# Cell stage of a two-layer block: selector rows in the free half, first split on VectorE, weighing ahead of scoring

## The chip, the cores and the metric

One NeuronCore of one Trainium2 chip runs the whole program in one launch. The metric is device time in microseconds (us) of that core. The engines are TensorE (PE), VectorE (DVE), ScalarE (ACT), GpSimd (POOL) and SyncE (SP, which only issues transfers here).

## The reference

Two transformer blocks at 512 tokens and width 1024, in fp32. The first has forgetting attention, chunked attention, memory attention and a gated feed forward; the second has an mLSTM layer, a multi-head latent attention layer and two squared-ReLU feed forwards. The change touches only the mLSTM mixer. Its recurrence over chunks is equal to one masked product over all 512 tokens, and that is what the kernel computes for each of 8 heads:

```
bb = cumsum(log_sigmoid(f));  m_t = running max over s<=t, in log space
w[t,s] = exp(bb_t - bb_s + i_s - m_t)   for s <= t, else 0
s[t,s] = (q_t . k_s) * w[t,s]
h_t    = sum_s s[t,s] v_s / max(|sum_s s[t,s]|, exp(-m_t))
out    = (rmsnorm(h) * sigmoid(og)) @ w_out
```

q and k have 64 columns per head, v has 128.

## The kernel before

All fp32 products are made of reduced-precision pieces: an operand is split into a high part (fp32r, rounded by ACT) and a low part (the difference), and `three` (L631 to L635) issues high x high, high x low and low x high. Weights come as 314 panels of 128x1024: SP loads a panel into `stage`, ACT makes `WH` (L1076), POOL makes `WL` (L528), PE uses them.

The cell stage lies between the projection "a_in" (queries, keys, output gate, values) and the projection "a_out". It runs over 8 heads n and, in each, over 4 blocks of 128 keys kb. A step is s = 4n + kb; its width is 512 - 128 kb query columns (512, 384, 256, 128), because later keys are seen by fewer queries. For each step:

- PE `cell_scores(s)` (L949): three matmuls of keys by queries into `G[s%2]`, contraction over 64 rows (rows 0 to 63 for an even head, 64 to 127 for an odd one); one matmul that spreads the head's running-maximum row, `SELC[0:40]` by `RB[0:40]`, into `T[s%2]` (L960); one matmul identity by `maskTr`, 128 columns (L961), which adds the causal mask.
- ACT `cell_exp(s)` (L1388): exponent of `T` into `sq`. DVE `cell_probs(s)` (L1928): `t` = `G` times `sq`.
- ACT `cell_pt_high(s)` (L1396) and then the low part of the weights into `CPT`: for kb = 0 on POOL (`first_low`, L576), else on DVE (`cell_pt_low`, L1934).
- PE `cell_weigh(s)` (L970): three matmuls of values by weights into `O[0]` (L633 to L635) and two of ones by weights into `O[1]` (L985), contraction over 128 rows.

Once for each head: PE `cell_guard` (L967, exp(-m) row, `SELC[64:104]` by `RB[64:104]`) and ACT `cell_guard_exp` (L1400); after the fourth weighing ACT `cell_square` (L1407 and L1410), DVE `cell_take` (L1941, frees `O[0]`), PE `cell_mean` (L993, two passes' worth of fp32 records), DVE `cell_den` (L1945) and `cell_sum` (L1950), ACT `cell_root` (L1414 logarithm, L1418 exponent), POOL `gate` (L581), DVE `cell_norm` (L1955), ACT `cell_high` (L1422), POOL `out_low` (L585). The banks `O[0]` and `O[1]` are single, so the first weighing of a head waits for `cell_take` and `cell_square` of the head before.

The order on each engine is written by hand; every engine works its list strictly from the front, and a wait blocks what is behind it. PE's list is in the code printed below. ACT's, for step s: [kb=1: square of head n-1], `pt_high(s)`, `exp(s+2)`, [kb=2: `guard_exp(n)`], [kb=3: `root(n-1)`], [kb=2: `high(n-2)`]. DVE's: [kb=1: `take(n-1)`], `probs(s+1)`, `pt_low(s)` (kb > 0), [kb=2: `den(n-1)`], [kb=3: `sum(n-1)`], [kb=1: `norm(n-2)`]. POOL's, for head n: `first_low(n)`, `out_low(n-2)`, `gate(n-1)`.

Behind the stage, `project` "a_out" starts with chunks 0 and 1, whose input rows are the heads' outputs, k = 0 to 6 first and k = 7 last. SP issues the load of the positions (into `apiece`, which overlaps `CW`) and the a_out panels 2 and on only when `out_low` of the last head is done.

## Time and profile before

| what | value |
|---|---|
| median of 3 runs | 2446.33 us (2441.97 to 2459.98) |
| profiled execution | 2446.78 us, of which the span from the first to the last instruction is 2445.0 us |
| mean granted TensorE clock over the span | 0.952 |
| PE / DVE / ACT / POOL busy | 92% / 48% / 36% / 40% |

A busy PE is not a PE at full rate: TensorE is granted 1.2 or 2.4 GHz, and the view of stretches prints the mean of that as a share of 2.4 GHz (0.50 is 1.2 GHz). Timeline rows give start, duration, engine, line, operation, output<-input and shape; in brackets stands the idle time of the engine before the row and who ended it. Matmul records overlap, because they are pipelined: the distance between two starts is what a matmul costs in a stream.

### The profile page before, as it was taken

Reading aid. Unit: us, or ns where it says so; the run is one execution under the profiler, and the core shown is the slowest. Engines: PE = TensorE matmul, PEld = TensorE weight load, DVE = VectorE, ACT = ScalarE, POOL = GpSimd, SP = SyncE. Lnnn points to the kernel's source line nnn. Section 1 sums busy time; section 2 is a strip of 40 time slices with the busy share of each in tenths; the row PEclk is TensorE's granted clock in tenths of the full one; section 3 lists DMA queues with packets and bytes.
Section 4 is the critical chain, followed back from the end, with each engine's and each line's share of the span. In section 5 each row is a group of like instructions: output and inputs, shape, how many; then the busy total and the mean of one; then the engine's idle time right before and its main releaser. Section 6 shows DMA issues by size and latency. Waiting matters only on the chain.

```text
span 2445.0 us, 27598 instructions
## 1 busy us (share of the span) xinstructions
PE 2245.8 (92%) x9514; PEld 1728.7 (71%) x9514; DVE 1174.7 (48%) x1669; ACT 888.8 (36%) x1449; POOL 976.9 (40%) x499
## 2 busy tenths in 40 slices
PE   6999968699899999899998899999977998999997
PEld 4777756577688888576666688888655776888885
DVE  4745544523555556763444643343553336434435
ACT  4226653343322222333344433223345444322332
POOL 2436624453344444333323344444324543444443
PEclk9999979799999999999868999999989899999999
DMA  5750022211144444255201122222212001222222
GB/s 194 254 192 18 7 98 86 78 60 61 52 155 154 161 158 154 103 198 174 76 1 48 51 95 94 94 94 94 69 44 69 26 27 49 91 92 93 94 94 78
DMA packets 66599, 234.25 MB, mean 96 GB/s; under 512 B 7136, under 2 KB 8416, under 8 KB 66400
## 3 DMA queue, kind: packets, MB, share of 16 engines
q1 hardware_dynamic: 66528, 233.33, 28.6%
q8 instruction: 41, 0.67, 0.1%
q14 instruction: 30, 0.25, 0.0%
HBM read 231.20 MB, written 2.10 MB: 95 GB/s over the span
## 4 chain that ended last, share of the span: by engine, by line
PE 76%; issue 8%; DVE 7%; ACT 5%; POOL 3%; DMA 1%; SPq 0%; POOLq 0%; DVEq 0%; ACTq 0%
PE bank L633 24%; PE bank L635 22%; PE bank L634 22%; POOL WL L528 2%; PE bank L705 2%; DVE acc L1554 1%; DVE Y L1579 1%; PE bank L748 1%; ACT sq L1090 1%; DVE H L1575 1%; DVE apiece L1629 1%; DMA apiece<-ada 1%; ACT WH L1076 1%; DVE Y L1618 1%; PE bank L690 1%
## 5 line engine op out<-in xcount | busy, mean ns | idle before, releaser
L528 POOL TENSOR_TENSOR WL<-stage,WH 128x1024 fp32r<-128x1024 f32 x314 | 763.7, 2433 | 1233.8 <-ACT WH L1076 1233.8
L1076 ACT ACTIVATE WH<-stage 128x1024 fp32r<-128x1024 f32 x314 | 332.6, 1060 | 1108.3 <-PE bank L635 1072.2
L633 PE MATMUL bank<-H,WH 128*128 128x512 f32 x1524 | 616.8, 405 | 58.3 <-DVE H L1575 32.2
L634 PE MATMUL bank<-H,WH 128*128 128x512 f32 x1524 | 608.6, 399 | 0.0
L635 PE MATMUL bank<-H,WL 128*128 128x512 f32 x1524 | 608.6, 399 | 0.0
L633 PEld LDWEIGHTS bank<-H,WH 128*128 128x128 f32 x1524 | 290.0, 190 | 156.0 <-issue 43.3
L635 PEld LDWEIGHTS bank<-H,WL 128*128 128x128 f32 x1524 | 290.0, 190 | 70.6
L634 PEld LDWEIGHTS bank<-H,WH 128*128 128x128 f32 x1524 | 290.7, 191 | 66.6 <-issue 0.8
L633 PE MATMUL bank<-HID,WH 128*128 128x512 f32 x688 | 272.9, 397 | 5.2 <-DVE Y L1758 5.2
L1758 DVE TENSOR_TENSOR Y<-bank,Y 128x512 f32<-128x512 f32 x344 | 226.0, 684 | 107.6 <-PE bank L635 106.5
L634 PE MATMUL bank<-HID,WH 128*128 128x512 f32 x688 | 272.8, 397 | 0.0
L635 PE MATMUL bank<-HID,WL 128*128 128x512 f32 x688 | 272.7, 396 | 0.0
L1629 DVE SCALAR_TENSOR_TENSOR apiece<-apiece,cond 128x1024 f32<-128x1024 f32 x112 | 189.2, 1703 | 108.3 <-DMA apiece<-ada 108.2
L1744 DVE SCALAR_TENSOR_TENSOR t<-bank,t 128x512 f32<-128x512 f32 x64 | 44.3, 692 | 286.3 <-ACT t L1230 286.2
L1748 DVE TENSOR_TENSOR HID<-t,HID 128x512 fp32r<-128x512 f32 x86 | 125.8, 1462 | 66.5 <-ACT HID L1235 66.5
L633 PEld LDWEIGHTS bank<-HID,WH 128*128 128x128 f32 x688 | 129.8, 189 | 36.9 <-issue 5.6
L635 PEld LDWEIGHTS bank<-HID,WL 128*128 128x128 f32 x688 | 129.7, 189 | 31.5
L634 PEld LDWEIGHTS bank<-HID,WH 128*128 128x128 f32 x688 | 129.7, 189 | 31.3
L1554 DVE TENSOR_TENSOR acc<-acc,sq 128x512 f32<-128x512 f32 (+1 forms) x59 | 89.7, 1520 | 101.0 <-ACT sq L1090 100.7
L1703 DVE TENSOR_TENSOR PT<-bank,PT 128x128 fp32r<-128x128 f32 (+2 forms) x112 | 54.0, 482 | 78.3 <-ACT PT L1190 78.1
L556 POOL TENSOR_SCALAR sq<-sq,stat 128x384 f32<-128x384 f32 (+2 forms) x56 | 74.2, 1336 | 21.1 <-DVE stat L1696 21.1
L1690 DVE TENSOR_REDUCE stat<-bank 128x1 f32<-128x128 f32 (+2 forms) x112 | 53.6, 479 | 50.0 <-PE bank L815 21.7
(257 smaller groups left out, 2777.0 us busy)
## 6 DMA issues: line engine op xcount, KB each, us to landing
stage<-panels SPq DMA_DIRECT2D x314, 512.0 KB, 3.5
apiece<-ada SPq DMA_DIRECT2D x112, 512.0 KB, 4.3
x<-xT SPq DMA_DIRECT2D x4, 1024.0 KB, 6.9
outT<-x SPq DMA_DIRECT2D x8, 256.0 KB, 2.1
Y<-bias SPq DMA_DIRECT2D x1, 1024.0 KB, 4.8
V<-memT SPq DMA_DIRECT2D x2, 512.0 KB, 4.4
con<-cons SPq DMA_DIRECT2D x1, 517.0 KB, 6.3
cond<-c SPq DMA_DIRECT2D x1, 512.0 KB, 9.1
```

The lines of the kernel that those rows point to most:

```text
L528: pool.tensor_tensor(WL[:, slot, :], stage[:, slot, :], WH[:, slot, :].bitcast(F32), ALU.subtract).then_inc(s_split, 1)
L556: pool.tensor_scalar(prob[qb][:, 0:w], prob[qb][:, 0:w], stat[:, 8 + qb:9 + qb], None, ALU.mult)\
L633: pe.matmul(out, wh, rh, start=start, stop=False)
L634: pe.matmul(out, wh, rl, start=False, stop=False)
L635: return pe.matmul(out, wl, rh, start=False, stop=stop)
L1076: act.activation(WH[:, slot, :], stage[:, slot, :], ACT.Copy).then_inc(s_hisplit, 1)
L1554: dve.tensor_tensor(acc[:, 0:width], first, sq[:, m % 2, 0:width], ALU.add).then_inc(s_add, 1)
L1629: dve.scalar_tensor_tensor(apiece[:, k % 2, :], apiece[:, k % 2, :], 1.0, cond[:], ALU.mult, ALU.mult, accum_out=adac[:, column]).then_inc ...
L1690: dve.tensor_reduce(stat[:, qb:qb + 1], score_bank[qb][:, 0:keys_of(name, qb)], AX, ALU.max, negate=True)\
L1703: dve.tensor_tensor(lo, T[qb % 2][:, 0:w].rearrange("p (k q) -> p k q", q=P), hi.bitcast(F32), ALU.subtract).then_inc(sm["pt_split"], 1)
L1748: dve.tensor_tensor(HID[:, slot, j, 1, :], t[:, j, :], HID[:, slot, j, 0, :].bitcast(F32), ALU.subtract).then_inc(sm["split"], 1)
L1758: dve.tensor_tensor(Y[:, m, :], (T + O)[m % 4][:, :], Y[:, m, :], ALU.add)\
```

## The change

1. **Free half.** The selector matmul of `cell_scores` takes `SELC` and `RB` rows of the half that the head's keys don't use: rows 64 to 103 for an even head, 0 to 39 for an odd one. It is issued second, between the first and the second key matmul. So `RB[64:104]` now holds a copy of the maximum rows, and the guard rows move to a new tile `RG` (rows 0 to 39). To make room, `wgate` is placed over `V`, `maskTr` goes (the one mask tile `maskr` is rewritten before and after the cells), `MR` goes.
2. **First split on DVE.** `first_low` leaves POOL; `cell_pt_low` runs for all four kb on DVE. `cell_norm` leaves DVE for POOL, whose list is now `gate(n)`, `norm(n)`, `out_low(n)`, head by head.
3. **PE order.** In each step PE issues `cell_weigh(s-1)`, then the mean if it is due, then `cell_scores(s+2)`, then the guard; before, `cell_scores(s+2)`, guard, mean, `cell_weigh(s-1)`.
4. **Warm matmuls.** In each of the first two steps four matmuls of 512 columns into `O[1]` are added, whose result nobody uses (`warm`, L687), and PE waits for all value low parts ahead of the loop.

ACT's list in the cells is unchanged. The diff, cut to what the prediction speaks of:

```diff
@@ -571,27 +570,24 @@
             def cells():
-                def first_low(n):
-                    pool.wait_ge(cell["pt_high"], 4 * n + 1)
-                    pool.tensor_tensor(CPT[:, 1, 0, :], t[:, 0, :], CPT[:, 0, 0, :].bitcast(F32), ALU.subtract)\
-                        .then_inc(cell["pt_low_first"], 1)
-
                 def gate(n):
                     pool.wait_ge(cell["root"], n + 1)
                     pool.tensor_tensor(rstd[:, :], rstd[:, :], QK[:, 8 + n, :], ALU.mult).then_inc(cell["gated"], 1)
+
+                def norm(n):
+                    pool.wait_ge(cell["gated"], n + 1)
+                    pool.tensor_tensor(CW[:, 2 + n % 2, :], CW[:, 2 + n % 2, :], rstd[:, :], ALU.mult)\
+                        .then_inc(cell["normed"], 1)
                 def out_low(n):
                     pool.wait_ge(cell["high"], n + 1)
                     pool.tensor_tensor(H[:, n, 1, :], CW[:, 2 + n % 2, :], H[:, n, 0, :].bitcast(F32), ALU.subtract)\
                         .then_inc(cell["split"], 1)
-                for n in range(HEADS + 2):
-                    if n < HEADS:
-                        first_low(n)
-                    if n >= 2:
-                        out_low(n - 2)
-                    if 1 <= n <= HEADS:
-                        gate(n - 1)
+                for n in range(HEADS):
+                    gate(n)
+                    norm(n)
+                    out_low(n)
             split_lows(0, PANEL0["mem_k"] + 2)
             attention("self")
...
@@ -955,29 +952,31 @@
                     pe.wait_ge(s_vlow, NT + 2)
                 if s >= 2:
                     await_bank_pair(pe, s)
-                three(G[s % 2][:, 0:w], QKH[rows, 4 + n // 2, keys], QKL[rows, 4 + n // 2, keys],
-                      QKH[rows, n // 2, kb * P:S], QKL[rows, n // 2, kb * P:S], True, True)
-                pe.matmul(T[s % 2][:, 0:w], SELC[0:40, n * P:(n + 1) * P], RB[0:40, kb * P:S], start=True, stop=False)
-                pe.matmul(T[s % 2][:, 0:P], identr[:, :], maskTr[:, :], start=False, stop=True)\
-                    .then_inc(cell["scores"], 1)
+                gates, out = gate_rows[1 - n % 2], T[s % 2]
+                sel = SELC[gates, n * P:(n + 1) * P]
+                kh, kl = QKH[rows, 4 + n // 2, keys], QKL[rows, 4 + n // 2, keys]
+                qh, ql = QKH[rows, n // 2, kb * P:S], QKL[rows, n // 2, kb * P:S]
+                pe.matmul(G[s % 2][:, 0:w], kh, qh, start=True, stop=False)
+                pe.matmul(out[:, 0:w], sel, RB[gates, kb * P:S], start=True, stop=False)
+                pe.matmul(G[s % 2][:, 0:w], kh, ql, start=False, stop=False)
+                pe.matmul(G[s % 2][:, 0:w], kl, qh, start=False, stop=True)
+                pe.matmul(out[:, 0:P], identr[:, :], maskr[:, :], start=False, stop=True).then_inc(cell["scores"], 1)
             def cell_guard(n):
                 if n:
                     pe.wait_ge(cell["guard_exp"], n)
-                pe.matmul(AD[:, :], SELC[64:104, n * P:(n + 1) * P], RB[64:104, :], start=True, stop=True)\
+                pe.matmul(AD[:, :], SELC[0:40, n * P:(n + 1) * P], RG[:, :], start=True, stop=True)\
                     .then_inc(cell["guard"], 1)
             def cell_weigh(s):
                 n, kb = s // 4, s % 4
+                pe.wait_ge(cell["pt_low"], s + 1)
                 if kb == 0:
-                    pe.wait_ge(cell["pt_low_first"], n + 1)
                     if n:
                         pe.wait_ge(cell["num"], n)
                         pe.wait_ge(cell["den_square"], n)
                     else:
                         pe.wait_ge(s_vlow, 2 * NT)
-                else:
-                    pe.wait_ge(cell["pt_low"], 3 * n + kb)
                 at = slice(n * P, (n + 1) * P)
                 three(O[0][:, kb * P:S], VH[:, kb, at], VL[:, kb, at],
                       CPT[:, 0, kb, kb * P:S], CPT[:, 1, kb, kb * P:S], kb == 0, kb == NT - 1)
...
@@ -994,15 +993,18 @@
             cell_scores(0)
             cell_scores(1)
+            pe.wait_ge(s_vlow, 2 * NT)
             for s in range(4 * HEADS):
+                if s < 2:
+                    warm(O[1], 4)
+                if s:
+                    cell_weigh(s - 1)
+                if s % 4 == 2 and s >= 4:
+                    cell_mean(s // 4 - 1)
                 if s + 2 < 4 * HEADS:
                     cell_scores(s + 2)
                 if s % 4 == 0:
                     cell_guard(s // 4)
-                if s % 4 == 2 and s >= 4:
-                    cell_mean(s // 4 - 1)
-                if s:
-                    cell_weigh(s - 1)
             cell_weigh(4 * HEADS - 1)
             cell_mean(HEADS - 1)
...
@@ -1371,13 +1373,14 @@
             evacuate_high("a_in", lambda c: QKH[:, c, :], lambda c: 1.0 if c // 4 % 2 else 64 ** -0.5)
             evacuate("a_og", 8, lambda c: QK[:, c + 8, :], func=ACT.Sigmoid)
             load_ln_exp()
+            act.activation(maskr[:], con[:, CON["maskT"]:CON["maskT"] + P], ACT.Copy).then_inc(s_cr, 1)
             logit_rows(1, 16)
             evacuate_half(PANEL0["a_in"] + 16, 0, 1, VH)
             act.wait_ge(s_scan, 1)
+            act.activation(RB[64:72, :], t[0:8, 0, :], ACT.Copy)
             act.activation(RB[0:8, :], t[0:8, 0, :], ACT.Copy).then_inc(s_rb, 1)
             act.wait_ge(s_scan, 2)
-            act.activation(RB[64:72, :], CW[0:8, 2, :], ACT.Copy)
-            act.activation(MR[:, :], CW[0:8, 2, :], ACT.Copy).then_inc(s_rb, 1)
+            act.activation(RG[0:8, :], CW[0:8, 2, :], ACT.Copy).then_inc(s_rb, 1)
             evacuate_half(PANEL0["a_in"] + 16, 1, None, VH)
             def cell_exp(s):
...
@@ -1908,8 +1913,9 @@
             chain.link(dve.tensor_copy(gs[:], ST[:, 0:8 * NT].rearrange("p (a b) -> p a b", b=8)))
             dve.wait_ge(s_rb, 2)
             dve.tensor_tensor(RB[32:40, :], t[0:8, 0, :], RB[0:8, :].bitcast(F32), ALU.subtract)
+            dve.tensor_tensor(RB[96:104, :], t[0:8, 0, :], RB[0:8, :].bitcast(F32), ALU.subtract)
             dve.wait_ge(s_rb, 3)
-            dve.tensor_tensor(RB[96:104, :], CW[0:8, 2, :], MR[:, :].bitcast(F32), ALU.subtract).then_inc(s_rbl, 1)
+            dve.tensor_tensor(RG[32:40, :], CW[0:8, 2, :], RG[0:8, :].bitcast(F32), ALU.subtract).then_inc(s_rbl, 1)
             for n in range(HEADS):
                 last = dve.tensor_scalar(SELC[:, n * P:(n + 1) * P], ones[0:104, :],
                                          con[0:104, CON["minus_onehot"] + n:CON["minus_onehot"] + n + 1], None,
...
@@ -1920,10 +1926,7 @@
             def cell_probs(s):
                 n, kb = s // 4, s % 4
                 if s >= 2:
-                    if (s - 2) % 4 == 0:
-                        dve.wait_ge(cell["pt_low_first"], (s - 2) // 4 + 1)
-                    else:
-                        dve.wait_ge(cell["pt_low"], (s - 2) // 4 * 3 + (s - 2) % 4)
+                    dve.wait_ge(cell["pt_low"], s - 1)
                 dve.wait_ge(cell["exp"], s + 1)
                 dve.tensor_tensor(t[:, s % 2, 0:S - kb * P], G[s % 2][:, 0:S - kb * P], sq[:, s % 2, 0:S - kb * P],
                                   ALU.mult).then_inc(cell["probs"], 1)
...
@@ -1949,11 +1952,6 @@
                 dve.wait_ge(cell["mean"], n + 1)
                 dve.scalar_tensor_tensor(CW[:, n % 2, :], ST[:, :], 1.0 / P, CW[:, n % 2, :], ALU.mult, ALU.add)\
                     .then_inc(cell["sum"], 1)
-
-            def cell_norm(n):
-                dve.wait_ge(cell["gated"], n + 1)
-                dve.tensor_tensor(CW[:, 2 + n % 2, :], CW[:, 2 + n % 2, :], rstd[:, :], ALU.mult)\
-                    .then_inc(cell["normed"], 1)
             steps = 4 * HEADS
             cell_probs(0)
...
@@ -1963,14 +1961,12 @@
                     cell_take(n - 1)
                 if s + 1 < steps:
                     cell_probs(s + 1)
-                if kb and s < steps:
+                if s < steps:
                     cell_pt_low(s)
                 if kb == 2 and 1 <= n <= HEADS:
                     cell_den(n - 1)
                 if kb == 3 and 1 <= n <= HEADS:
                     cell_sum(n - 1)
-                if kb == 1 and n >= 2:
-                    cell_norm(n - 2)
             dve.wait_ge(s_pos, 16)
             chain.link(dve.tensor_copy(ropeF, apiece[:].bitcast(I32)[:, 0, 0:S]))
```

## Rows read from the trace of the kernel before

**Rows 1.** View of stretches: us, busy of PE, PEld, DVE, ACT, POOL, clock, DMA share, GB/s.

```profile
1204.00:1308.60 104.60, 97.65 (x342) 66.49 (x342) 48.74 (x86) 52.06 (x109) 27.05 (x22) 0.69 0.00 1
...
1236.00:1239.00 3.00, 3.00 (x7) 1.54 (x7) 1.03 (x3) 0.62 (x2) 0.00 (x0) 0.50 0.03 5
```

**Rows 2.** Timeline of PE: a head's first weighing, first and last of seven.

```profile
1221.11 0.47 PE L633 MATMUL bank<-CPT,VH 128*128 128x512 f32 x1 [0.79 <-DVE CW L1941]
...
1301.72 0.79 PE L633 MATMUL bank<-CPT,VH 128*128 128x512 f32 x1 [1.90 <-POOL CPT L576]
```

**Rows 3.** Timeline of ACT, from the exponent of step 28 to the square.

```profile
1293.85 0.69 ACT L1388 ACTIVATE sq<-bank,gs 128x512 f32<-128x512 f32 x1 [3.52 <-PE bank L961]
...
1295.01 0.63 ACT L1422 ACTIVATE H<-CW 128x512 fp32r<-128x512 f32 x1
1295.53 0.31 ACT L1396 ACTIVATE CPT<-t 128x128 fp32r<-128x128 f32 x1
...
1297.79 0.63 ACT L1414 ACTIVATE logs<-CW 128x512 f32<-128x512 f32 x1 [0.58 <-DVE CW L1950]
1298.45 0.63 ACT L1418 ACTIVATE rstd<-logs 128x512 f32<-128x512 f32 x1
1298.98 0.61 ACT L1396 ACTIVATE CPT<-t 128x512 fp32r<-128x512 f32 x1
...
1299.86 0.59 ACT L1407 ACTIVATE acc<-bank 128x512 f32<-128x512 f32 x1
```

**Rows 4.** Timelines of DVE and POOL in the cell stage.

```profile
1227.22 0.29 DVE L1934 TENSOR_TENSOR CPT<-t,CPT 128x128 fp32r<-128x128 f32 x1
...
1295.87 1.28 DVE L1934 TENSOR_TENSOR CPT<-t,CPT 128x128 fp32r<-128x128 f32 x1 [0.53 <-ACT CPT L1396]
1297.07 0.68 DVE L1950 SCALAR_TENSOR_TENSOR CW<-bank,CW 128x512 f32<-128x512 f32 x1
...
1300.48 0.75 DVE L1941 TENSOR_SCALAR CW<-bank,vec 128x512 f32<-128x512 f32 x1 [2.27 <-ACT acc L1407]
...
1295.72 1.29 POOL L585 TENSOR_TENSOR H<-CW,H 128x512 fp32r<-128x512 f32 x1 [7.92 <-ACT H L1422]
1299.16 1.28 POOL L581 TENSOR_TENSOR rstd<-rstd,QK 128x512 f32<-128x512 f32 x1 [2.15 <-ACT rstd L1418]
```

**Rows 5.** Timeline of PE: matmuls that open a step's parts.

```profile
1223.15 0.79 PE L633 MATMUL bank<-QKH 64*128 64x512 f32 x1
...
1225.43 2.02 PE L993 MATMUL bank<-acc,con 128*128 128x512 f32 x2
...
1263.12 0.79 PE L633 MATMUL bank<-QKH 64*128 64x512 f32 x1
...
1264.97 2.02 PE L993 MATMUL bank<-acc,con 128*128 128x512 f32 x2
...
1268.51 0.69 PE L633 MATMUL bank<-QKH 64*128 64x384 f32 x1
...
1288.00 0.47 PE L633 MATMUL bank<-QKH 64*128 64x128 f32 x1
...
1289.59 0.77 PE L633 MATMUL bank<-CPT,VH 128*128 128x512 f32 x1
...
1291.99 0.79 PE L633 MATMUL bank<-QKH 64*128 64x512 f32 x1
1292.00 0.79 PE L960 MATMUL bank<-RB,SELC 40*128 40x512 f32 x1
...
1293.59 1.07 PE L993 MATMUL bank<-acc,con 128*128 128x512 f32 x2
...
1295.48 0.44 PE L633 MATMUL bank<-QKH 64*128 64x384 f32 x1
```

**Rows 6.** View of waits in the cell stage: us in total, times, longest.

```profile
PE bank L633 <- POOL CPT L576: 5.8, 5, 1.9
```

**Rows 7.** Chain of waits behind the cells: start, us, what.

```profile
1315.96 7.43 issue
```

More of the change, by code:

```diff
@@ L178, in program @@
         maskr = sb("maskr", [P, P], F32R)
-        maskTr = sb("maskTr", [P, P], F32R)
-        wgate = sb("wgate", [P, KC, 24])
         wgateH = sb("wgateH", [P, KC, 24], F32R)
@@ L196, in program @@
         RB = sb("RB", [104, S], F32R)
+        RG = sb("RG", [40, S], F32R)
         def place(at, name, shape, dt=F32):
@@ L213, in program @@
         CW = place(32, "CW", [P, 4, S])
-        MR = place(38, "MR", [8, S], F32R)
         CPT = place(16, "CPT", [P, 2, NT, S], F32R)
@@ L226, in program @@
         V = place(104, "V", [P, NT, D])
+        wgate = place(104, "wgate", [P, KC, 24])
         VH = place(104, "VH", [P, NT, D], F32R)
@@ L373, in program @@
         cell = {k: sem(f"cell_{k}") for k in (
-            "scores", "exp", "probs", "pt_high", "pt_low_first", "pt_low", "pv", "guard", "guard_exp", "den",
+            "scores", "exp", "probs", "pt_high", "pt_low", "pv", "guard", "guard_exp", "den",
             "den_square", "num", "square", "mean", "sum", "log", "root", "gated", "normed", "high", "split")}
@@ L946, in _ @@
             pe.wait_ge(s_selc, 1)
+            pe.wait_ge(s_cr, 2)
             freed(pe, "a_in", 8)
@@ L1055, in _ @@
             pe.wait_ge(s_rql, 4)
+            pe.wait_ge(s_cr, 3)
             attention("mla", mla_scores, lambda qb: qb + 1, causal_pv, before(VTILES, "kv_b") + 2 * NT + 1)
@@ L1298, in _ @@
             act.activation(onesr[:], ones, ACT.Copy)
-            act.activation(maskr[:], con[:, CON["mask"]:CON["mask"] + P], ACT.Copy)
-            act.activation(maskTr[:], con[:, CON["maskT"]:CON["maskT"] + P], ACT.Copy).then_inc(s_cr, 1)
+            act.activation(maskr[:], con[:, CON["mask"]:CON["mask"] + P], ACT.Copy).then_inc(s_cr, 1)
             act.wait_ge(s_c, 16)
@@ L1440, in _ @@
                     cell_high(n - 2)
+            act.activation(maskr[:], con[:, CON["mask"]:CON["mask"] + P], ACT.Copy).then_inc(s_cr, 1)
             evacuate_squares("a_out", "a")
@@ L1808, in _ @@
             make_scaled("x", xc, vcol("g_mix_pre"), hl, zero)
+            dve.memset(RG[:].bitcast(F32), 0.0)
             dve.memset(RB[:].bitcast(F32), 0.0).then_inc(s_pad, 1)
```

## The prediction

> **What bounds the kernel now.** I read the page first: PE is busy for most of the span, so time is won or lost where PE waits or runs at its low clock. Then I looked only at the cell stage, since the diff touches little else. The view of stretches says what kind of stage it is: of 104.6 us PE is busy 97.7, yet the mean clock is 0.69, which means some 62% of the time at 1.2 GHz [rows 1]. A stretch without any idle can be at 0.50 as well. So there are two costs: waits, and the low clock, which sets in around the waits at the head boundaries and goes again some 7 us later.
>
> Then the period of a head, from the first weighing of one head to that of the next. Six of them take 1301.72 - 1221.11 = 80.61 us, 13.43 each [rows 2]. The releasers named there and in the view of waits are `take` on DVE and `first_low` on POOL, with 5.8 us for five waits on POOL [rows 2, 6]. That is what the change goes for.
>
> But what stands behind POOL? In the last full head I split the period at the exponent of step 4n+4 on ACT. From there to the next head's first weighing, 1293.85 to 1301.72, it is 7.87 us, and PE idles 1.90 at its end, so this part was no longer set by PE [rows 2, 3]. I call it B. The reader should follow it as a chain [rows 3, 4]: exponent, guard exponent, `high`, the high part of step 4n+3 (begins 1295.53), its low part on DVE (ends 1297.15), `sum` (1297.07 to 1297.75), logarithm (1297.79), exponent (1298.45), high part of the next head's first block (1298.98), exponent of step 4n+6, square (1299.86), `take` (1300.48 to 1301.23). All of this is hand order on ACT and DVE. The change leaves ACT's list as it is.
>
> **The change, part by part.**
>
> *PE order, the decisive part.* Call A the stretch from the first weighing of a head, W(4n), to the exponent of step 4n+4. Before, PE issued in A: W(4n), then the scores S(4n+4), because S(4n+3) had gone ahead of W(4n) and the mean and W(4n+1) came behind. After, the list is W(4n), S(4n+3), W(4n+1), mean, S(4n+4). Three pieces move in front of the exponent with which B begins. Nothing overlaps A with the B of the same head: ACT can't get at the chain of B before it has done that exponent, and PE can't pass W(4n) before `take` at the end of B. So a period is A + B.
>
> At 1.2 GHz A is: W(4n) 1291.99 - 1289.59 = 2.40; S(4n+3) at most 1289.59 - 1288.00 = 1.59; mean with W(4n+1) 1268.51 - 1264.97 = 3.54; S(4n+4) with the selector overlapped 1264.97 - 1263.12 = 1.85; and 0.26 from the last matmul to the exponent (1293.85 against 1293.59) [rows 3, 5]. Sum 9.64. At 2.4 GHz mean with W(4n+1) is 1295.48 - 1293.59 = 1.89, a factor of 0.53; the other pieces by that factor are 3.10, so A is 1.89 + 3.10 + 0.26 = 5.25. The idle at the end of B stands right before A, and that is where the clock fell before, so I take A nearer its upper end, with the stage's 62 to 65% at 1.2 GHz: 5.25 + 0.65 x 4.39 = 8.1 us.
>
> *First split on DVE.* POOL's 1.28 us drop out of the chain. The low part now starts on DVE when the high part is done (1299.6 in the example), but at that time POOL runs `gate`, 1299.16 to 1300.44, and this subtraction has two inputs in SBUF. What that does is in the trace: a low part of 128 columns takes 0.29 us alone and 1.28 beside POOL's `out_low`, ending 0.14 after it (1297.15 against 1297.01) [rows 4]. A low part of 512 columns lasts about 0.4 more than one of 128 (0.68 for an operation of that size against 0.29), so it would end 0.54 after `gate`, at 1300.98. `take`, behind it on DVE, lasts 0.75, and W(4n+4) begins at about 1301.75, where it began before. So B stays 7.9 to 8.0: the wait on POOL changes its name. The other end: `norm` is now queued on POOL right behind `gate`. If it got in before the waiting DVE, another 1.28 would come on top, B = 9.2. `norm` first waits for `gate`'s own semaphore while DVE is already waiting, so I take 8.0.
>
> The Trainium skill (SBUF — State Buffer, on the port pair shared by VectorE and GpSimd) says that an operation with two SBUF inputs and a GpSimd operation exclude each other for the whole instruction. By that rule this edit wins nothing at the boundary; if the two were free to overlap, B would be about 0.5 shorter and the sum 3 us less. The trace agrees, by the 1.28 against 0.29.
>
> `norm` on POOL costs 1.28 instead of 0.68 there; in mid stage `high` waits for it a head later and it is hidden by A. DVE and POOL are idle for half of the stage [rows 1].
>
> *Free half.* For an odd head the selector already starts with the first key matmul (1291.99 and 1292.00) [rows 5]. For an even one it stands in line: 1225.43 - 1223.15 = 2.28 against 1.85, so 0.43 for 512 columns at 1.2 GHz, about 1.07 for a head's 1280 columns. Only S(4n+4) of that lies in A (it is in the 1.85 above); the rest lies in B, where PE now waits anyway.
>
> The Trainium skill (TensorE: Matmul & The Clock Gate, Part 3) has matmuls start strictly in program order. By that rule the odd heads would gain from issuing the selector second too, some 0.43 each; the two starts 10 ns apart, for a matmul that is issued fourth, speak against it, and I count nothing.
>
> *Periods.* A + B = 16.1 us against 13.43. The first of the six has no `high` and no `out_low`, so it is some 0.52 + 0.98 shorter. Six periods: 6 x 2.67 - 1.5 = +14.5 us.
>
> *Start.* Eight warm matmuls at 0.43 (the 512-column difference above) are 3.4 us at 1.2 GHz; four shorter selectors in head 0 give 1.07 back. The high clock may come a little sooner. I take +2, between 0 and 3.4. The added wait for the values' low parts costs nothing: they are done before the scores of step 1 end.
>
> *End.* In the last head the low part of step 31 now waits behind its exponent, guard exponent, `high` and POOL's `out_low`, with only weighing work on PE to cover it: +2. `norm` on POOL adds 1.28 - 0.68 = 0.6 to the closing chain, at whose end the transfers of the positions and of the next panels are issued; PE's wait for them follows (7.43 us from `out_low` to the first low part) [rows 7]. It all shifts: +2.6.
>
> *Small edits at nothing.* The zeroing of `RG`, one more 8-row subtraction, the copies of mask and rows: they run beside the projections on DVE and ACT. Without that cover they would be about 1 us in all. The low parts of kb > 0 and the guard have the same durations as before.
>
> Sum, against the profiled execution's own 2446.8 us (the span 2445.0 and 1.8 around it, 0.5 above the median of the runs): 2446.8 + 14.5 + 2 + 2.6 = 2465.9, say **2466 us**.
>
> **Rivals.**
>
> *The clock holds (0.12).* If PE stays at 2.4 GHz in spite of the longer idle, A is 5.25 and the period 13.2: 6 x (-0.2) - 1.5, start 0, end +2: about 2446. [...] Against it: the idle per head grows to 3 or 4 us at that clock, and waits of about 1 us were enough before.
>
> *The chain gets longer (0.17).* A wholly at 1.2 GHz and `norm` or another POOL operation ahead of DVE now and then: 9.64 + 8.0 to 8.5 gives 17.6 to 18.1, +24 to +27, with 3.4 and 3 for the ends 2477 to 2480, and up to 2485 with the full 1.28 in five heads.
>
> *Faster (0.09).* The other side: PE sets the pace again. Then the 5.8 us of waits on POOL go and four even heads save 1.07 each: about 2437. With the clock at 2.4 GHz throughout, a head would be some 8 us (0.53 of the 15 that it takes at 1.2) and the total 2416. This decides from the point where B falls below 13.43 - 8.1 = 5.3 us. In its favour: only that the boundary waits were named by POOL and DVE. Against: every link of B in rows 3 and 4 is still there, in the same order.
>
> **How the numbers follow.** The forecast has 0.62, with a range of its own of 2456 to 2474. The clock that holds has 0.12, the longer chain 0.17, faster 0.09. The range 2447 to 2482 leaves out the faster side and the ends. More or less than 1% of 2446.3, about what a measurement can tell from no change, is 24.5 us: slower by more than that needs 2470.8, which is most of the longer chain and a seventh of the forecast, 0.26; faster by more, 0.04; between, 0.70.
>
> **What would show it.** Periods between a head's first weighings of about 16 us, of which the part from ACT's 512-column exponent to the next first weighing is 7.9 to 8.3. Idle of PE ahead of the first weighing of 1.5 to 2.5 us, put down to `take`, and a second idle ahead of the fourth weighing (128 columns), put down to DVE's low part. DVE's first low part stretched to over 1 us beside `gate`. Even heads' scores of 512 columns at 1.85 us at 1.2 GHz. Clock in the stage at 0.60 to 0.70. I'd be wrong if B came out short, if the idle at the boundary vanished, or if the clock in the stage rose above 0.85.

## The result, and the profile after

The kernel after takes 2469.3 us (median of 10 executions, 2461.45 to 2476.64), against 2446.65 us of the kernel before beside it: ratio 1.009, 95% interval 1.0073 to 1.0107. The forecast was 2466 with a range of 2447 to 2482. The profiled execution of after took 2466.59 us, its span is 2464.8.

The stretches of after's timeline come first: the whole cell stage, and the six periods from the first weighing of head 1 to that of head 7 (us; busy time of PE, PEld, DVE, ACT, POOL; clock; DMA share; GB/s).

```profile
1202.60:1330.30 127.70, 108.11 (x350) 73.11 (x350) 54.21 (x88) 51.35 (x108) 25.90 (x19) 0.61 0.00 1
1221.97:1321.31 99.34, 81.62 (x258) 54.55 (x259) 42.12 (x67) 39.94 (x84) 23.25 (x17) 0.60 0.00 0
```

Six periods take 99.34 us, 16.56 each, where they took 80.61 [rows 2]. PE is busy 81.62 of them and idle 17.72. In the same six periods of before the view of stretches has 74.69 busy, so 5.92 idle: 11.8 us of the 18.7 are idle, and 6.9 are matmuls that take longer, because the clock is 0.60 instead of 0.69.

One period in PE's timeline, from the first weighing of head 5 to that of head 6:

```profile
1287.44 0.76 PE L629 MATMUL bank<-CPT,VH 128*128 128x512 f32 x1 [1.22 <-DVE CW L1944]
...
1289.84 0.47 PE L959 MATMUL bank<-QKH 64*128 64x128 f32 x1
...
1290.94 0.63 PE L629 MATMUL bank<-CPT,VH 128*128 128x384 f32 x1
...
1292.64 1.91 PE L992 MATMUL bank<-acc,con 128*128 128x512 f32 x2
1294.48 0.79 PE L959 MATMUL bank<-QKH 64*128 64x512 f32 x1
...
1296.13 0.33 PE L629 MATMUL bank<-CPT,VH 128*128 128x256 f32 x1
...
1299.72 0.48 PE L629 MATMUL bank<-CPT,VH 128*128 128x128 f32 x1 [1.81 <-DVE CPT L1937]
...
1304.33 0.77 PE L629 MATMUL bank<-CPT,VH 128*128 128x512 f32 x1 [1.23 <-DVE CW L1944]
```

This is the order that the change writes: weighing, scores of 128 columns, weighing, mean, and only then the scores of 512 columns. Two idles stand in the period: 1.81 us ahead of the 128-column weighing, put down to DVE's low part, and 1.23 ahead of the first weighing, put down to `take`. The view of waits in the stage adds them up:

```profile
PE bank L629 <- DVE CW L1944: 10.2, 7, 2.4
PE bank L629 <- DVE CPT L1937: 9.4, 6, 1.8
```

POOL has gone from this list [rows 6], and 19.6 us stand in it, where before had 5.8 on POOL and 0.8 on `take`. (One of the seven waits on `take` and one of the six on the low part lie ahead of the six periods.) What holds DVE is seen on ACT, DVE and POOL, from the 512-column exponent to `take`. These are their timelines, one after the other:

```profile
1296.39 0.69 ACT L1391 ACTIVATE sq<-bank,gs 128x512 f32<-128x512 f32 x1 [4.48 <-PE bank L963]
...
1297.55 0.63 ACT L1425 ACTIVATE H<-CW 128x512 fp32r<-128x512 f32 x1
1298.07 0.31 ACT L1399 ACTIVATE CPT<-t 128x128 fp32r<-128x128 f32 x1
...
1300.30 0.63 ACT L1417 ACTIVATE logs<-CW 128x512 f32<-128x512 f32 x1 [1.45 <-DVE CW L1953]
1300.96 0.63 ACT L1421 ACTIVATE rstd<-logs 128x512 f32<-128x512 f32 x1
1301.50 0.61 ACT L1399 ACTIVATE CPT<-t 128x512 fp32r<-128x512 f32 x1
...
1302.86 0.59 ACT L1410 ACTIVATE acc<-bank 128x512 f32<-128x512 f32 x1
...
1298.41 1.25 DVE L1937 TENSOR_TENSOR CPT<-t,CPT 128x128 fp32r<-128x128 f32 x1 [0.53 <-ACT CPT L1399]
1299.59 0.68 DVE L1953 SCALAR_TENSOR_TENSOR CW<-bank,CW 128x512 f32<-128x512 f32 x1
...
1302.14 1.34 DVE L1937 TENSOR_TENSOR CPT<-t,CPT 128x512 fp32r<-128x512 f32 x1 [1.41 <-ACT CPT L1399]
1303.48 0.75 DVE L1944 TENSOR_SCALAR CW<-bank,vec 128x512 f32<-128x512 f32 x1
...
1298.25 1.26 POOL L584 TENSOR_TENSOR H<-CW,H 128x512 fp32r<-128x512 f32 x1 [10.52 <-ACT H L1425]
...
1301.67 1.27 POOL L575 TENSOR_TENSOR rstd<-rstd,QK 128x512 f32<-128x512 f32 x1 [2.15 <-ACT rstd L1421]
1303.01 1.60 POOL L579 TENSOR_TENSOR CW<-CW,rstd 128x512 f32<-128x512 f32 x1
```

It is the chain of [rows 3, 4], link by link, with DVE's 1.34 beside `gate` in the place of POOL's first split. ACT stands idle for 4.48 us ahead of it: the exponent's scores are not there yet.

The clock in the same period, from the view of stretches: at its low level through nearly all of A, at the high one from the scores of 512 columns on, and low again before the idle ahead of the 128-column weighing is over.

```profile
1287.44:1295.75 8.31, 8.31 (x21) 5.31 (x21) 1.97 (x5) 0.68 (x3) 0.29 (x1) 0.50 0.00 0
1295.85:1299.20 3.35, 2.06 (x12) 1.42 (x11) 1.48 (x2) 2.45 (x5) 0.95 (x1) 1.00 0.00 0
1299.35:1304.33 4.98, 3.39 (x11) 2.45 (x12) 3.57 (x6) 3.63 (x7) 2.75 (x3) 0.50 0.01 2
```

### The profile page after: what moved, and what is told of

The parts are those of the page before. It is cut to its first block, busy times and chain, and to the rows that moved or that the text cites. A ratio compares the mean times of both kernels' runs of the same rounds, so it can differ in the third digit from the quotient of the medians.

```text
span 2464.8 us, 27617 instructions
## 1 busy us (share of the span) xinstructions
PE 2256.1 (92%) x9522; PEld 1736.1 (70%) x9522; DVE 1180.2 (48%) x1671; ACT 888.0 (36%) x1450; POOL 979.8 (40%) x499
## 4 chain that ended last, share of the span: by engine, by line
PE 75%; issue 8%; DVE 8%; ACT 5%; POOL 2%; DMA 1%; SPq 0%; POOLq 0%; DVEq 0%; ACTq 0%
PE bank L629 23%; PE bank L631 22%; PE bank L630 22%; POOL WL L527 2%; PE bank L701 2%; DVE acc L1558 1%; DVE Y L1583 1%; PE bank L744 1%; ACT sq L1093 1%; DVE H L1579 1%; DVE apiece L1633 1%; DVE Y L1622 1%; DMA apiece<-ada 1%; ACT WH L1079 1%; PE bank L686 1%
## 5 line engine op out<-in xcount | busy, mean ns | idle before, releaser
L686 PE MATMUL bank<-onesr,identr 128*128 128x512 f32 x288 | 82.2, 434 | 0.0
```

Source lines behind the costliest of these rows:

```text
L686: pe.matmul(out[:, :], identr[:, :], onesr[:, :].rearrange("p (a b) -> p a b", a=1).to_broadcast([P, 4, P]), start=True, stop=True)
```

## The experiments

In the table, "six periods" is the stretch from the first weighing of head 1 to that of head 7 in the profiled execution, with PE's busy time and the clock in it; "start" is from the first scores to head 1's first weighing. Those columns come from one execution, and there PE's clock and busy time can differ by 10 us in two kernels whose medians agree (e7 and e12). Most executions of a kernel lie within 10 us of its median, and the farthest, but for one of e9's told below, 23 above it (e6), so verdicts rest on the ratios, each to the kernel before as run beside it (2445.64 to 2449.19).

| kernel | median us | ratio to before (95%) | six periods | PE busy, clock | start |
|---|---|---|---|---|---|
| before | 2446.65 | | 80.61 | 74.69, 0.69 | 17.09 |
| after | 2469.3 | 1.009 (1.0073 to 1.0107) | 99.34 | 81.62, 0.60 | 19.35 |
| e1_old_order | 2447.31 | 0.9996 (0.9978 to 1.0014) | 78.29 | 71.15, 0.71 | 23.57 |
| e2_order_only | 2472.14 | 1.0094 (1.0067 to 1.012) | 100.57 | 84.60, 0.60 | 21.38 |
| e6_no_warm | 2468.66 | 1.0114 (1.0076 to 1.0152) | 99.88 | 86.72, 0.55 | 19.42 |
| e3_high_early | 2462.22 | 1.0064 (1.004 to 1.0088) | 94.65 | 83.36, 0.57 | 19.34 |
| e4_fill | 2466.76 | 1.0072 (1.0048 to 1.0095) | 90.27 | 76.88, 0.75 | 23.01 |
| e5_mean_boundary | 2454.29 | 1.0036 (1.0019 to 1.0054) | 86.33 | 76.16, 0.66 | 22.73 |
| e9_cure_new_order | 2434.60 | 0.9958 (0.994 to 0.9975) | 68.56 | 61.67, 0.84 | 19.84 |
| e7_cure | 2419.64 | 0.9887 (0.9862 to 0.9912) | 62.87 | 62.87, 0.80 | 20.09 |
| e8_cure_dve | 2417.95 | 0.9859 (0.9832 to 0.9887) | 53.88 | 53.88, 0.96 | 20.13 |
| e12_cure_selector_last | 2423.26 | 0.9889 (0.9862 to 0.9916) | 52.57 | 52.57, 0.99 | 19.98 |
| e11_cure_warm | 2425.72 | 0.9894 (0.9862 to 0.9925) | 54.62 | 54.62, 0.94 | 23.56 |
| e10_cure_on_before | 2432.92 | 0.9916 (0.9884 to 0.9949) | 68.63 | 68.47, 0.75 | 20.20 |

### Which part costs the time

My theory was that the order on PE costs all of it, and that the free half and the split on DVE only change names. The rival was that DVE's stretched low part or `norm` on POOL costs.

**e1_old_order** is the kernel after with PE's list put back:

```diff
             for s in range(4 * HEADS):
                 if s < 2:
                     warm(O[1], 4)
-                if s:
-                    cell_weigh(s - 1)
-                if s % 4 == 2 and s >= 4:
-                    cell_mean(s // 4 - 1)
                 if s + 2 < 4 * HEADS:
                     cell_scores(s + 2)
                 if s % 4 == 0:
                     cell_guard(s // 4)
+                if s % 4 == 2 and s >= 4:
+                    cell_mean(s // 4 - 1)
+                if s:
+                    cell_weigh(s - 1)
```

> The changed kernel with PE's order in a step put back (scores of step s+2, guard, mean, then the weighing of step s-1); free half, first split and norm placement, and the warm matmuls stay. Order theory: the loss is the three pieces (scores of step 4n+3, weighing of step 4n+1, mean) that stand between a head's first weighing and ACT's 512-column exponent. Without them that part A falls from 8.7 to some 4.1 us, the period from 16.6 to about 13, and the time to 2443 to 2450. Rival, the loss is in the splits and norm moved between DVE and POOL: the time stays above 2460.

**e2_order_only** is the kernel before with only the reverse of that edit.

> The kernel before with only PE's order in a step changed. Order theory: A rises to about 8.7 us and the period to 16.5, time 2463 to 2468, of which the missing 2 to 3 us against the changed kernel are the warm matmuls and norm on POOL. Rival: under 2455, if the order costs only together with the other parts.

Measured: 0.9996 and 1.0094. The first interval holds 1, the second covers the whole effect of the change. In e1 A is 2.65 to 4.56 us and B 7.9 to 11.0; in e2 A is 8.3 to 9.6 and B 7.9 to 8.2 from head 2 on. So the order alone costs the 0.9%, and everything else in the change adds up to nothing, within some 0.2%. e2 still has POOL's first split and its B is the same as after's, which is the case for "the wait changes its name".

**e6_no_warm** leaves out the eight warm matmuls (`if s < 2: warm(O[1], 4)`).

> The changed kernel without the eight warm matmuls at the start of the cells. By my start term they cost about 2 us: from the first scores to head 1's first weighing 17.3 instead of 19.35 us, time about 2467. Rival: they pay for themselves in the clock of head 0 and the time goes up by 2 or more.

Measured 2468.66, no gain. Its start is 19.42 us and after's 19.35, though after has eight matmuls more in it, 3.4 us by the working of the prediction. The clock is 0.54 here and 0.70 in after's. The two starts in the view of stretches, e6's first:

```profile
1208.30:1227.72 19.42, 17.78 (x57) 12.21 (x58) 8.16 (x16) 8.40 (x18) 1.09 (x1) 0.54 0.00 0
...
1202.62:1221.97 19.35, 17.52 (x66) 11.81 (x66) 8.16 (x16) 8.40 (x18) 1.09 (x1) 0.70 0.00 0
```

It is not shown that the warm matmuls bring that clock. e3, e4 and e5 have them too, with after's program up to what stands ahead of head 1's first weighing. Between the first weighings of heads 0 and 1 the clock is 0.82 in after and in e3, and 0.50 in e4, e5 and e6. So with the same matmuls it rose in head 0 in two profiled executions and not in two others.

### What the period is made of

If the period is A + B, then a link taken out of either shortens it by that link.

**e3_high_early** moves `high` of two heads back from the far side of the 512-column exponent to step 4n+1 on ACT:

```diff
                 if s + 2 < steps:
                     cell_exp(s + 2)
+                if kb == 1 and n >= 2:
+                    cell_high(n - 2)
...
-                if kb == 2 and n >= 2:
-                    cell_high(n - 2)
```

> The changed kernel with one thing moved in ACT's list: high(n-2) from behind guard_exp(n) to behind the exponent of step 4n+3, where ACT is idle. Chain theory: B, from ACT's 512-column exponent to the next first weighing, loses the 0.52 of high and the 0.96 by which POOL's out_low stretches the 128-column low part, so 7.94 becomes about 6.5 in five heads, and the time falls by 7 us to about 2462. Rival, PE sets B: B and the time do not move by more than 2 us.

Measured 2462.22, the time that was expected, but B fell less than the 1.4 of the expectation. From 7.94 it goes to 7.25, or to 6.4 in the two heads where PE runs it at 2.4 GHz (clock 0.90 and 0.91 there, 0.50 in the others). At the low clock it falls no further because the next link is PE: in ACT's timeline of head 2 the 384-column exponent, which stands ahead of the logarithm, now waits for its scores.

```profile
1256.38 0.58 ACT L1391 ACTIVATE sq<-bank,gs 128x384 f32<-128x384 f32 x1 [1.37 <-PE bank L963]
1256.86 0.62 ACT L1417 ACTIVATE logs<-CW 128x512 f32<-128x512 f32 x1
```

**e5_mean_boundary** takes the mean out of A. It is issued ahead of W(4n), where PE waits anyway:

```diff
-                if s:
-                    cell_weigh(s - 1)
-                if s % 4 == 2 and s >= 4:
-                    cell_mean(s // 4 - 1)
+                if s % 4 == 1 and s >= 4:
+                    cell_mean(s // 4 - 1)
+                if s:
+                    cell_weigh(s - 1)
```

> The changed kernel with the mean of the head before issued ahead of a head's first weighing (in PE's wait for take) and no longer behind its second. One of the three pieces leaves A. Order theory: A falls by the 1.7 us that the mean takes at 1.2 GHz, B grows by up to 0.9 because the square that the mean needs is done only 0.9 us before the weighing; net about 1.2 a head, time about 2462. If A is set by something else than the sum of its pieces, the time stays at 2469.

Measured 2454.29, 8 us better than expected. The mean itself is 1.84 us of A (1294.48 - 1292.64 above), but a part of it still runs into the first weighing. In heads 2 and 3, at 0.50 throughout, A is 7.99 and 8.14, where e6 has 9.20 at that clock, and B is 0.25 longer, so the piece alone gives back about 1 us a head. The larger part is the clock: in the last three heads A is 5.6 to 5.8, with a clock of 0.75 in such a period, where after has 8.8 to 9.0 at 0.60.

**e4_fill** keeps PE busy instead. Four warm matmuls go into the mean's bank ahead of each first weighing from head 1 on:

```diff
+                if s in range(5, 32, 4):
+                    if s >= 8:
+                        pe.wait_ge(cell["sum"], s // 4 - 1)
+                    warm(ST, 4)
                 if s:
                     cell_weigh(s - 1)
```

> The changed kernel with four more warm matmuls of 512 columns ahead of each head's first weighing (from head 1), into the bank of the mean, which is free there. They lie in PE's wait for take. Chain theory: B stays at 7.9 and only the clock can change A; I expect little, 2460 to 2470. Rival, the low clock after the boundary's idle is the main cost: the clock in the stage rises from 0.61 to above 0.8, A falls from 8.7 toward 5.3, and the time to about 2450.

Measured 2466.76: the interval overlaps after's, so no gain is shown. The clock did rise, to 0.75 over the six periods, and they took 90.27 us instead of 99.34. Of that gain 3.7 us went into a longer start, and the medians show none of it. The clock alternates. Two neighbouring periods in the view of stretches:

```profile
1292.41:1309.75 17.34, 15.52 (x48) 10.64 (x48) 7.83 (x13) 6.77 (x14) 4.52 (x4) 0.60 0.00 0
1309.75:1323.14 13.39, 10.72 (x48) 6.99 (x47) 6.53 (x11) 6.66 (x14) 3.78 (x3) 0.88 0.01 2
```

At 0.88 a period is 13.39, A 5.52 and B 7.87. These are the values of my rival "the clock holds" (5.25, period 13.2), in two heads. They say that even there the new order only equals before's 13.43 at 0.69, since the chain of B takes its 7.9 us at either clock: 7.87 here, and 7.94 in e6 in periods that are at 0.50 from end to end. In the periods at 0.60 the added matmuls make B longer, 8.52.

### Taking the chain apart

If ACT's and DVE's hand order holds B at 8 us, moving its links must bring PE back as the bound.

**e7_cure** does that in the old order of PE. The mean and `sum` are done a step or two earlier, `root` (logarithm and exponent) goes ahead of the 512-column exponent, where ACT had idled, and `high` behind it at step 4n+1. No warm matmuls. The rest of the change stays. Against the kernel after:

```diff
@@ PE
-                if s < 2:
-                    warm(O[1], 4)
-                if s:
-                    cell_weigh(s - 1)
-                if s % 4 == 2 and s >= 4:
-                    cell_mean(s // 4 - 1)
                 if s + 2 < 4 * HEADS:
                     cell_scores(s + 2)
                 if s % 4 == 0:
                     cell_guard(s // 4)
+                if s % 4 == 1 and s >= 4:
+                    cell_mean(s // 4 - 1)
+                if s:
+                    cell_weigh(s - 1)
@@ ACT
+                if kb == 2 and 1 <= n <= HEADS:
+                    cell_root(n - 1)
                 if s + 2 < steps:
                     cell_exp(s + 2)
+                if kb == 1 and n >= 2:
+                    cell_high(n - 2)
                 if kb == 2 and n < HEADS:
                     cell_guard_exp(n)
-                if kb == 3 and 1 <= n <= HEADS:
-                    cell_root(n - 1)
-                if kb == 2 and n >= 2:
-                    cell_high(n - 2)
@@ DVE
-                if kb == 2 and 1 <= n <= HEADS:
+                if kb == 1 and 1 <= n <= HEADS:
                     cell_den(n - 1)
-                if kb == 3 and 1 <= n <= HEADS:
                     cell_sum(n - 1)
```

> The changed kernel's parts with the order made for the chain: PE's order put back (scores ahead), mean of the head before ahead of a head's first weighing, no warm matmuls; DVE does den and sum right behind take's step (kb = 1); ACT does root at kb = 2 ahead of its 512-column exponent and high at kb = 1. Chain theory: root and sum leave the chain from exponent to the next first weighing, and out_low no longer stretches the 128-column low part, so B falls below what PE needs; period 9.5 to 11.5 instead of 13.4, time 2420 to 2435, faster than the kernel before. Rival, the stage is PE and its clock in any case: period stays near 13, time 2440 to 2450.

**e9_cure_new_order** is the same with weighing ahead of scores on PE, as the change has it.

> As the run before (mean ahead of the first weighing, early den, sum, root and high, no warm matmuls) but with the changed kernel's order on PE, weighing ahead of scores. Order theory: A still holds the scores of step 4n+3 and the second weighing, so the period is 1.5 to 3 us longer than with the scores ahead; time 2435 to 2450. Rival, the order is harmless once the chain is short: within 3 us of the run before.

Measured: e7 0.9887, e9 0.9958. Each median lies within half a us of the fast end of its range. (One of e9's twelve executions took 8549 us; I can't say why. The ratio leaves it out, and the median without it is 2434.44.) In e7 PE has no idle in the six periods, 62.87 busy of 62.87. B is 5.3 to 5.9 in the heads with a clock of 0.83 to 1.00 and 9.82 in the one at 0.50, and what limits it is PE itself. The new order still costs 15 us against the old one in the medians: in e9 PE idles 6.9 us of 68.56, A is 4.6 to 8.1. The profiled periods, 11.4 us in e9 and 10.5 in e7, differ by less than the 1.5 to 3 that I expected.

### What the parts of the change are worth once PE is the bound

**e10_cure_on_before** has the cure's moves in the kernel before: no free half, first split on POOL, `norm` on DVE.

```diff
-                if s % 4 == 2 and s >= 4:
+                if s % 4 == 1 and s >= 4:
                     cell_mean(s // 4 - 1)
```

(and the moves on ACT and DVE shown for e7)

> The kernel before with the cure alone (mean of the head before, `den`, `sum` at kb == 1, `root` ahead of the exponent at kb == 2, `high` at kb == 1): no free half, first split still on POOL, `norm` on DVE. Theory: the cure takes the chain apart and earns nearly all of the 27 us; what the change brings on top is the selector's overlap, 4.5 to 8.6 us (eight heads at 0.53 to 1.07), of which odd heads had theirs already, so 2422 to 2430. Rival: the first split on POOL (1.28, behind `out_low` on POOL's list) is then the last link of B in each head, seven times 0.6 to 1.3 more: 2428 to 2437. Second rival: the change's own parts earn nothing, 2419 to 2422.

**e8_cure_dve** is e7 with `norm` back on DVE.

```diff
+                if kb == 3 and 1 <= n <= HEADS:
+                    cell_norm(n - 1)
```

> e7_cure with `norm` taken back from POOL to DVE, at kb == 3 behind the low part of that step. If `norm` is hidden work wherever it stands, the time is that of e7_cure within 3 us (2417 to 2423). Rival: now that the stage is set by PE and B is only 5.3 to 5.9, a queue counts: on DVE the 0.68 stands ahead of the low part of step 4n, and B grows by up to 0.68 in each of seven heads, 2420 to 2425; or on POOL the 1.6 that it took beside DVE was what held DVE back, and then its return gives 2 to 5 us (2415 to 2418).

**e11_cure_warm** is e7 with the warm matmuls.

> e7_cure with the change's 8 warm matmuls ahead of steps 0 and 1. In e7_cure the first two heads run at 1.2 GHz with a period of 15.0 us, the next ones take 10. If the warm matmuls lift the clock for head 0 and it then holds, head 0 and 1 gain up to 4 us each, minus 1.7 to 3.4 for themselves: 2413 to 2418. If they only pay for themselves, as leaving them out of the changed kernel showed (2468.7 against 2469), 2418 to 2422.

**e12_cure_selector_last** is e7 with the selector issued fourth, in the free half:

```diff
                 pe.matmul(G[s % 2][:, 0:w], kh, qh, start=True, stop=False)
-                pe.matmul(out[:, 0:w], sel, RB[gates, kb * P:S], start=True, stop=False)
                 pe.matmul(G[s % 2][:, 0:w], kh, ql, start=False, stop=False)
                 pe.matmul(G[s % 2][:, 0:w], kl, qh, start=False, stop=True)
+                pe.matmul(out[:, 0:w], sel, RB[gates, kb * P:S], start=True, stop=False)
```

> e7_cure with the selector issued behind the three key matmuls again, but still in the other half of the rows. If matmuls start strictly in the order of issue and overlap only with their neighbour, the selector of 512, 384, 256 and 128 columns still overlaps with the third key matmul, and nothing changes: 2417 to 2423. If the place right behind the first key matmul is what lets it overlap, every head loses 0.53 (2.4 GHz) to 1.07 us (1.2 GHz), and since PE is busy 84 of 85 us it shows in full: 2424 to 2429.

Measured on one chip: e8 0.9859, e12 0.9889, e11 0.9894, e10 0.9916. e8's interval and e10's just meet; the other differences are not told apart. So the moves of the cure earn 0.8% on their own (0.5 to 1.2). Of the expectations e8's held, though 2417.95 lies at the edge of a rival's range too; e12's 2423.26 lies just above the first range and below the rival's, and e11's 2425.72 above both of its ranges. With the change's free half and first split the medians lie 7 to 15 us lower again, which only e8 bears out, and barely. e10's 2432.9 misses my first expectation (2422 to 2430). It lies in the range of the rival, but not for its reason: PE has no wait on POOL in the six periods. What it has is a lower clock, 0.75 against 0.99 in e12. PE is without idle in both but for 0.16 us in e10, so why the clock fell in the one I did not settle. e7 warns against making much of it: its matmuls are e12's but for the place of the selector, its clock was 0.80, its six periods took 10 us more, and the two ratios are alike. The place of `norm` and the warm matmuls give nothing that these runs can tell.

e12 answers on the selector. The stretch of five of its periods, and the scores of 512 columns in PE's timeline:

```profile
1237.82:1280.79 42.97, 42.97 (x217) 29.34 (x216) 29.76 (x56) 33.36 (x72) 21.16 (x15) 1.00 0.00 1
```

```profile
1247.80 0.49 PE L959 MATMUL bank<-QKH 64*128 64x512 f32 x1
1247.81 0.49 PE L962 MATMUL bank<-RB,SELC 40*128 40x512 f32 x1
1248.14 0.39 PE L960 MATMUL bank<-QKL,QKH 64*128 64x512 f32 x1
1248.37 0.39 PE L961 MATMUL bank<-QKH,QKL 64*128 64x512 f32 x1
1248.70 0.33 PE L963 MATMUL bank<-maskr,identr 128*128 128x128 f32 x1
```

L962 is issued fourth and starts 10 ns behind the first. From the first key matmul to the mask it is 0.90 us, and in e8, with the selector issued second, it is 0.90 too (1249.72 to 1250.62). In e10 an even head with the selector in its own half takes 1.13. So it is the free half that gives the overlap, and the place in the order gives nothing. A period is 42.97 / 5 = 8.59 us here, at 1.00 and without idle: PE's own time for a head at 2.4 GHz. At 1.2 GHz, also without idle, e7's first two heads take 14.3 and 15.0.

ACT's timeline of e12 shows why B no longer matters:

```profile
1249.14 0.63 ACT L1419 ACTIVATE rstd<-logs 128x512 f32<-128x512 f32 x1
1249.68 0.67 ACT L1389 ACTIVATE sq<-bank,gs 128x512 f32<-128x512 f32 x1
...
1251.51 0.62 ACT L1397 ACTIVATE CPT<-t 128x512 fp32r<-128x512 f32 x1
...
1253.53 0.60 ACT L1408 ACTIVATE acc<-bank 128x512 f32<-128x512 f32 x1 [0.59 <-PE bank L984]
```

From the exponent to the high part of the next head's first block it is 1.83 us, where after needs 5.11 (1296.39 to 1301.50). The square that `take` follows now waits for PE's last weighing of the head, and not PE for it.

## Why the prediction was right, point by point

**The order is the decisive part: right.** e2 makes the whole loss with it alone, and without it e1 has none. The period is A + B in every head, and the exponent starts 0.26 us after PE has gone on to the next piece (1296.39 against 1296.13). One thing the prediction did not say: the B of 7.87 that it read is the shortest of before's six, the others were 8.69 to 11.52 with A at 3.66 to 4.62. Over the six periods A grew by 27.6 us and B shrank by 8.8.

**B = 8.0, the wait on POOL changes its name: right.** It is 7.85 to 7.94 in heads 2 to 6. DVE's low part took 1.34 us beside `gate` and ended 0.54 after it (1303.48 against 1302.94), as worked out from the 128-column case. `norm` did not get in before the waiting DVE; it was the one held up, at 1.60 us. The Trainium skill (SBUF — State Buffer, "SBUF: two separate sides") has the pair held for a whole instruction by whichever of the two starts first. These rows agree.

**A = 8.1: too low, the term that was mis-sized most.** Its mean is 8.75, 0.65 more in six heads, 3.9 us. Piece by piece in the period shown: W(4n) 2.40, scores of 128 columns 1.10 (I had "at most 1.59"), weighing and mean 3.54, scores of 512 columns 1.65, and 0.26, in all 8.95. With 1.10 the bounds of A are 9.15 at 1.2 GHz and 4.99 at 2.4, and 8.75 means that 90% of it is at the low clock and not the stage's 62 to 65% that I took. The stage's mean was the wrong number for A, and the idle that the prediction named was not the one to look at. In four of the six periods the clock falls in the other idle, ahead of the 128-column weighing, as in the three stretches of the period shown. PE comes to A at the low clock, and gets the high one back only with the scores of 512 columns at A's end. Of the 3.35 us at 2.4 GHz in the second of those stretches it works for 2.06. The statement that the low clock goes again some 7 us after it sets in was too simple as well: in before that is so for four of seven stretches, and the others lasted 10 to 17 us.

**Six periods +14.5: +18.7.** 3.9 of the difference is A. The other 0.4 is B: without `high` and `out_low` I had the first one 1.5 shorter, at 6.5, and it was 7.27, which is 0.8 more; the five others give 0.4 back. What e3 shows holds in the first period too: past `high`, PE's scores of 384 columns are the next link.

**Start +2: 2.3 (19.35 against 17.09).** The size was right by luck. e6, without the warm matmuls that are 3.4 of it, has the same start at a lower clock, and whether the clock rises in head 0 changed between executions of the same matmuls.

**End +2.6: +2.8, for a partly wrong reason.** From the last head's first weighing to PE's first matmul that had waited for the panels it is 27.32 us (1321.31 to 1348.63), against 24.49. The last `out_low` starts 3.5 us later after that weighing (17.68 against 14.17), and 0.7 comes back behind it. I had put 0.6 of it down to `norm` on POOL. In the old order of PE it costs nothing: the last `out_low` is at 13.73 in e1 and 13.68 in e7 with `norm` on POOL, and at 13.62 in e8 with it on DVE. In e2, with the new order and no other part, it is at 16.80. So 2.6 of the 3.5 is the order, more than the 2 that I had; the other 0.9 is there only when the new order and the rest of the change come together, and was not taken apart.

**The sum.** 18.7 + 2.3 + 2.8 = 23.8, of which the profiled span shows 19.8: its stage began 1.4 us earlier, and what lies behind took 2.6 less, both places that the change doesn't touch. The medians differ by 22.7. That the profiled execution came within 1 us of the forecast is thus luck: the three terms were 4.7 us too low together, and 4.0 us elsewhere made up for it.

**The rivals.** "The clock holds" appears only where PE was given work at the boundary, in every other head of e4. "The chain gets longer" was the nearest to what came: its first half, A nearly wholly at 1.2 GHz, is what happened, its second half, B above 8, is not. "Faster" named the point from which PE sets the pace, B below 5.3, and the state beyond it, some 8 us a head and 2416 in all. The four cured kernels with the change's free half and the old order reach 2418 to 2426, at best with 8.59 a head. That B is 5.3 there too is chance: at the high clock it is PE's own work in that part, not the length of a chain. Of what would show it, all held: periods of about 16 (16.6), the two idles with their names, even heads' scores of 512 columns at 1.85 us (1229.02 to 1230.87), a clock of 0.60 to 0.70. Only the idle ahead of the first weighing was mostly shorter than I said, 1.2 to 1.5 and once 2.4.

## What to carry to other kernels

When two engines hand work to each other through hand-written lists, find the piece at which one's chain begins and count what the other's list puts ahead of it: weighing the older block first put three pieces ahead of the exponent that everything waited for, and that cost 18.7 us in six periods, where the waits that the change went for were 5.8. Look past the engine that a wait names to the first link of its chain that could have run earlier; here moving the logarithm, `high`, `sum` and the mean one or two steps forward took nothing away and made the kernel 0.8% faster alone, and 1.1 to 1.4% together with the change's free half and first split. And price a piece by the clock at which the engine will come to it, which an idle further ahead can have set, and not by the stage's mean.

## What the runs showed of the hardware

The matmul in the other half of the rows starts 10 ns behind the first key matmul when it is issued fourth, at no cost to the three between (e12). The Trainium skill (TensorE: Matmul & The Clock Gate, Part 3) has matmuls start strictly in program order; these rows differ, and the period of 8.59 us, the same as with the selector second, goes with the rows.

The low clock costs this stage at least as much as its waits do. After's PE is busy 81.6 us in six periods, before's 74.7, and e12's, which has the same matmuls as after in these periods, 52.6. So against e12 some 29 us of after's 99 are low clock and 18 are idle; against e7, whose PE is busy for 62.9, the low clock's part is 19. With the idle gone the clock stayed at 1.00 for five heads in e12 and in e8. But idle is not all that lowers it: in e7 and e10, with at most 0.2 us of idle in the six periods, it was 0.80 and 0.75, and what made the difference is not shown.

The eight warm matmuls earned nothing that the ratios could tell in either kernel. After and e6 have the same start with and without them; in the cured kernel the start is 23.56 with them (e11) and 20.09 without (e7), and the clock of the start is 0.54 and 0.52.
